# Moving a mixture-of-experts token gather and scatter from TensorE to indirect DMA through HBM

## The reference, cut to what matters

```python
def swiglu(h, wg, wu, wd):
    return (jax.nn.silu(h @ wg) * (h @ wu)) @ wd

def moe_swiglu(h, router, wg, wu, wd):          # h: (1, 256, 1024), wg, wu: (8, 1024, 3584), wd: (8, 3584, 1024)
    logits = (h @ router).astype(jnp.float32)
    top_val, top_idx = lax.top_k(logits, TOP_K)  # 2 of 8
    probs = jax.nn.softmax(top_val, axis=-1)
    combine = jnp.einsum('bske,bsk->bse', jax.nn.one_hot(top_idx, N_EXPERTS, dtype=jnp.float32), probs)
    out = jnp.zeros(h.shape, jnp.float32)
    for e in range(N_EXPERTS):
        out = out + combine[..., e:e + 1] * swiglu(h, wg[e], wu[e], wd[e]).astype(jnp.float32)
    return out.astype(h.dtype)
```

## Time and profile before

| | |
|---|---|
| median of 3 runs | 1943.22 us |
| profiled execution | 1944.21 us |
| its span | 1942.4 us |
| mean granted TensorE clock | 0.971 |
| PE, DVE, ACT busy over the span | 94%, 78%, 58% |
| HBM read, written | 483.31 MB, 1.05 MB |

### The profile page before, as it was taken

How to read it: one execution, slowest core, us unless ns; L and a number is a source line. 1 busy time by engine, 2 the same in 40 slices (tenths; PEclk the granted TensorE clock), 3 DMA queues, 4 the chain that set the end, 5 groups by cost and what they waited for, 6 DMA issues and landing times.

```text
span 1942.4 us, 27834 instructions
## 1 busy us (share of the span) xinstructions
PE 1817.0 (94%) x10592; PEld 1594.6 (82%) x10592; DVE 1521.2 (78%) x1487; ACT 1131.6 (58%) x923; POOL 5.1 (0%) x13
## 2 busy tenths in 40 slices
PE   6889899899988898897999999999999999999996
PEld 6888788799978897785788888888888888888885
DVE  3989967544548899576788989889898898988995
ACT  3345545444334355543576767777677776776774
POOL 0000000000000000000000000000000000000000
PEclk9999989999989999998899999999999999999998
DMA  6444333765334444335699999999999999999992
GB/s 235 137 146 153 130 98 129 249 195 186 117 122 143 136 141 148 109 131 184 215 381 338 359 359 364 363 340 357 363 362 353 348 360 377 344 355 347 369 367 90
DMA packets 234304, 485.51 MB, mean 250 GB/s; under 512 B 19040, under 2 KB 43616, under 8 KB 234096
## 3 DMA queue, kind: packets, MB, share of 16 engines
q1 hardware_dynamic: 233168, 479.65, 70.0%
q0 software_dynamic: 1056, 4.76, 0.6%
HBM read 483.31 MB, written 1.05 MB: 249 GB/s over the span
## 4 chain that ended last, share of the span: by engine, by line
PE 74%; DVE 19%; ACT 4%; DMA 2%; issue 1%; SPq 0%; DVEq 0%; ACTq 0%
PE pair L833 48%; PE aux L833 19%; DVE lo_ring L1315 6%; DVE arena L1378 5%; PE aux L1206 2%; ACT hi_ring L450 1%; PE pair L1228 1%; PE aux L1279 1%; DMA raw_ring<-in_w_in 1%; DVE arena L1547 1%; DVE arena L1496 1%; DVE arena L1482 1%; DVE small L1495 1%; DVE pair L1472 1%; DVE arena L1561 0%
## 5 line engine op out<-in xcount | busy, mean ns | idle before, releaser
L1315 DVE TENSOR_TENSOR lo_ring<-raw_ring,hi_ring 128x2048 fp32r<-128x2048 f32 (+2 forms) x278 | 623.3, 2246 | 139.0 <-ACT hi_ring L450 137.1
L450 ACT ACTIVATE hi_ring<-raw_ring 128x2048 fp32r<-128x2048 f32 (+2 forms) x278 | 522.5, 1881 | 298.5 <-PE pair L833 214.8
L1315 DVE TENSOR_TENSOR lo_ring<-arena,hi_ring 128x2048 fp32r<-128x2048 f32 x183 | 417.7, 2289 | 98.9 <-ACT hi_ring L450 97.4
L450 ACT ACTIVATE hi_ring<-arena 128x2048 fp32r<-128x2048 f32 x183 | 350.3, 1918 | 152.5 <-PE aux L833 81.4
L833 PE MATMUL pair<-hT_lo,hi_ring 128*128 128x256 f32 (+1 forms) x1360 | 396.5, 292 | 28.7 <-DVE lo_ring L1315 14.3
L833 PE MATMUL pair<-hT_hi,lo_ring 128*128 128x256 f32 (+1 forms) x1360 | 391.3, 288 | 0.0
L833 PE MATMUL pair<-hT_hi,hi_ring 128*128 128x256 f32 (+1 forms) x1360 | 391.1, 288 | 0.0
L833 PE MATMUL pair<-lo_ring,hT_hi 128*128 128x512 f32 x896 | 355.5, 397 | 3.9 <-DVE hT_lo L1820 2.4
L833 PE MATMUL pair<-hi_ring,hT_hi 128*128 128x512 f32 x896 | 350.1, 391 | 0.0
L833 PE MATMUL pair<-hi_ring,hT_lo 128*128 128x512 f32 x896 | 349.8, 390 | 0.0
L833 PEld LDWEIGHTS pair<-hT_lo,hi_ring 128*128 128x128 f32 (+1 forms) x1360 | 267.1, 196 | 36.4 <-issue 13.9
(11 more groups left out here) (285 smaller groups left out, 1895.8 us busy)
## 6 DMA issues: line engine op xcount, KB each, us to landing
raw_ring<-in_mu SPq DMA_DIRECT2D x222, 512.0 KB, 5.8
arena<-in_mg SPq DMA_DIRECT2D x220, 512.0 KB, 5.4
raw_ring<-in_w_in SPq DMA_DIRECT2D x120, 512.0 KB, 4.5
arena<-in_md SPq DMA_DIRECT2D x114, 512.0 KB, 5.5
raw_ring<-in_md SPq DMA_DIRECT2D x110, 512.0 KB, 5.5
raw_ring<-in_w_br SPq DMA_DIRECT2D x32, 512.0 KB, 4.5
raw_ring<-in_w_out SPq DMA_DIRECT2D x16, 512.0 KB, 4.2
raw_ring<-in_fg SPq DMA_DIRECT2D x12, 512.0 KB, 4.1
```

Of the source, the lines that this page charges most:

```text
L450: nc.scalar.activation(hi_ring[:, h, 0:cols], raw(slot)[:, 0:cols], ACT.Copy).then_inc(hi_ready, 1)
L1315: nc.vector.tensor_tensor(lo_ring[:, h, 0:cols], raw(slot)[:, 0:cols], hi_ring[:, h, 0:cols].bitcast(f32), ALU.subtract).then_inc(lo_ready, 1)
```

## The change

All rounds but the first now take their tokens out of HBM, and all but the last give their result to HBM. Two tensors of 384 rows x 1024 are added in HBM: `rows` (the 256 normed tokens and 128 spare rows) and `sums` (x, and 128 spare rows), filled from SBUF by four DMAs on the POOL queue after the last norm. `fetch(j)` on POOL is an indirect DMA that reads 128 rows of `rows` into `arena` (`A_ROWS`); `put(j)` is an indirect DMA that adds 128 rows of `arena` (`A_OUT`) into `sums`. The row numbers of each round are one column of `place`. A token position that no token fills points to a spare row. TensorE turns the fetched rows with 8 transposes (`turn_rows`) in step 5 instead of the gather, and DVE scales the round's result by its weights out of `aux` into `A_OUT` in step 1 (`output`), with no split, scatter or add. Before the last scatter, `sums` is read back into x.

The row numbers are found once: DVE makes the 0/1 matrices of all 12 slots (24 compares, L1877 of the changed kernel), TensorE multiplies them by a three-column table of token number, one and weight (`index_slots`, 24 matmuls in float32, after the first `exp_up`), and DVE turns the result into `place` and `wts` (`places`, four small operations). The last round keeps the old way out: `turn_pick`, `pickT_copy`, output split and scatter, now once, with the second token block's scatter going to `pair0` instead of waiting for `aux`.

The diff, cut to its core:

```diff
+A_ROWS, A_OUT = 7680, 8704
+A_PICKS = A_OUT
+ROWS = T + 128
...
+            pool.wait_ge(S["normed"], 8)
+            pool.dma_start(rows_d[0:T, :].rearrange("(b p) d -> p b d", p=128), hN).then_inc(rows_kept, 16)
+            pool.dma_start(sum_d[0:T, :].rearrange("(b p) d -> p b d", p=128), x[:, :, :]).then_inc(rows_kept, 16)
+            pool.dma_start(rows_d[T:ROWS, :], x[:, 0, :]).then_inc(rows_kept, 16)
+            pool.dma_start(sum_d[T:ROWS, :], x[:, 0, :]).then_inc(rows_kept, 16)
+
+            def fetch(j):
+
+                nc.gpsimd.tensor_copy(place_in[:, :], place[:, bass.ds(j, 1)]).then_inc(S["place_in_set"], 1)
+                pool.wait_ge(S["place_in_set"], j)
+                pool.sem_inc(pool_ready, 1)
+                pool.indirect_dma_start(ar(A_ROWS, D), None, rows_d, bass.IndirectOffsetOnAxis(ap=place_in[:, :], axis=0))\
+                    .then_inc(rows_in, 16)
+
+            def put(j):
+
+                nc.gpsimd.tensor_copy(place_out[:, :], place[:, bass.ds(j, 1)]).then_inc(S["place_out_set"], 1)
+                pool.wait_ge(S["place_out_set"], j + 1)
+                pool.wait_ge(S["out_scaled"], j + 1)
+                pool.sem_inc(pool_ready, 1)
+                pool.indirect_dma_start(sum_d, bass.IndirectOffsetOnAxis(ap=place_out[:, :], axis=0), ar(A_OUT, D), None,
+                                        compute_op=ALU.add).then_inc(sums_added, 16)
+
+            pool.wait_ge(rows_kept, 64)
+            pool.wait_ge(S["places_done"], 1)
+            fetch(1)
+
+            def slot(j):
+                pool.wait_ge(S["gathered"], j + 1)
+                fetch(j + 1)
+                if not (isinstance(j, int) and j == 1):
+                    pool.wait_ge(sums_added, 16 * j - 16)
+                put(j - 1)
+
+            slot(1)
+            with pool.Fori(2, NE) as j:
+                slot(j)
+            pool.wait_ge(S["meta_done"], 1)
+            m = pool.value_load(meta[0:1, 0:1], min_val=0, max_val=EXTRA)
+            with pool.If(m > 0):
+                with pool.Fori(NE, m + NE) as j:
+                    slot(j)
+            pool.wait_ge(sums_added, 16 * m + 16 * (NE - 1))
+            pool.sem_inc(pool_ready, 1)
+            pool.dma_start(x[:, :, :], sum_d[0:T, :].rearrange("(b p) d -> p b d", p=128)).then_inc(sums_in, 16)
...
-                    if s == 1 and not first:
-                        output_hi(j - 1, EXP_BASE + exp_at(j * EXP_STEPS, 5) + 1)
...
-                    if s == 3:
-                        pickT_copy(j)
...
+            pickT_copy()
+            output_hi(EXP_BASE + exp_at(exp_end, 1) + 1)
...
-            def gather(j):
-
-                pe.wait_ge(S["pick_done"], j + 1)
+            def gather_first():
+
+                pe.wait_ge(S["pick_done"], 1)
                 for k in range(KT):
                     for b in range(NB):
                         for n, src in enumerate((act_lo, act_hi)):
                             ins = pe.matmul(aux[:, 1024 + k * 128:1024 + (k + 1) * 128], src[:, b * D + k * 128:b * D + (k + 1) * 128],
                                             pick[:, b, :], start=(b == 0 and n == 0), stop=(b == 1 and n == 1))
+                ins.then_inc(S["gathered"], 1)
+
+            def index_slots():
+
+                pe.wait_ge(S["picks_done"], 1)
+                for c in range(SLOTS):
+                    for b in range(NB):
+                        ins = pe.matmul(aux[:, 1024 + 3 * c:1027 + 3 * c], ar(A_PICKS + (c * NB + b) * 128, 128),
+                                        ar(A_SCORE + 240 + (b * SLOTS + c) * 3, 3), start=(b == 0), stop=(b == 1))
+                ins.then_inc(S["indexed_slots"], 1)
+
+            def turn_rows(j):
+                pe.wait_ge(rows_in, 16 * j)
+                for k in range(KT):
+                    ins = pe.transpose(aux[:, 1024 + k * 128:1024 + (k + 1) * 128], ar(A_ROWS + k * 128, 128), C("ident"))
...
-            def turn_pick(j, first):
-                if not first:
-                    pe.wait_ge(S["x_added"], 2 * j)
+            def turn_pick():
+                pe.wait_ge(S["pick_done"], 2)
                 for b in range(NB):
-                    ins = pe.matmul(aux[:, 1024 + b * 128:1152 + b * 128], pick[:, b, :], ident_r[:, :], start=True, stop=True)
+                    ins = pe.matmul(pairs[0][:, b * 128:(b + 1) * 128], pick[:, b, :], ident_r[:, :], start=True, stop=True)
...
+                    if s == 0 and first:
+                        index_slots()
+                    if s == 5:
+                        turn_rows(j + 1)
                     if s == 1 and not first:
-                        scatter(j - 1, 0)
-                    if s == 3:
-                        turn_pick(j, first)
-                    if s == 5:
-                        pe.wait_ge(S["pickT_done"], j + 1)
-                        gather(j + 1)
+                        pe.wait_ge(S["out_scaled"], j)
                     if s:
                         exp_down(n, 4, s - 1)
                     elif not first:
                         exp_down(n, 4, EXP_STEPS - 1)
...
-                    if s == 1 and not first:
-                        scatter(j - 1, 1)
                     exp_turn(n)
 
-            def scatter(j, b):
-
-                if b == 0:
-                    pe.wait_ge(S["oe_lo_done"], j + 1)
-                else:
-                    pe.wait_ge(S["x_added"], 2 * j + 1)
-                for half in range(2):
-                    for n, src in enumerate((oel, oeh)):
-                        ins = pe.matmul(aux[:, 1024 + half * 512:1536 + half * 512], pickT[:, b, :],
-                                        src[:, half * 512:(half + 1) * 512], start=(n == 0), stop=(n == 1))
-                ins.then_inc(S["scattered"], 1)
+            def scatter():
+
+                pe.wait_ge(S["oe_lo_done"], 1)
+                pe.wait_ge(S["pickT_done"], 1)
+                for b in range(NB):
+                    for half in range(2):
+                        out = aux[:, 1024 + half * 512:1536 + half * 512] if b == 0 else pairs[0][:, half * 512:(half + 1) * 512]
+                        for n, src in enumerate((oel, oeh)):
+                            ins = pe.matmul(out, pickT[:, b, :], src[:, half * 512:(half + 1) * 512], start=(n == 0), stop=(n == 1))
+                    ins.then_inc(S["scattered"], 1)
...
+            turn_pick()
             exp_down((m + NE) * EXP_STEPS, 0, EXP_STEPS - 1)
-            scatter(m + (NE - 1), 0)
-            scatter(m + (NE - 1), 1)
+            scatter()
...
+            for c in range(SLOTS):
+                for b in range(NB):
+                    ins = nc.vector.tensor_scalar(ar(A_PICKS + (c * NB + b) * 128, 128), C("iota"), pos_t[:, b, c:c + 1], None,
+                                                  ALU.is_equal)
+            tok = ar(A_SCORE + 240, NB * SLOTS * 3).rearrange("p (b c k) -> p b c k", b=NB, k=3)
+            at = CONSTS["place"][0]
+            for b in range(NB):
+                nc.vector.tensor_copy(tok[:, b, :, 0:1], consts[:, at + b:at + b + 1].unsqueeze(1).broadcast_to([128, SLOTS, 1]))
+            nc.vector.memset(tok[:, :, :, 1:2], 1.0)
+            nc.vector.tensor_copy(tok[:, :, :, 2:3], comb_t[:, :, :].unsqueeze(3)).then_inc(S["picks_done"], 1)
...
-                        output_lo(j - 1)
-                    if s == 4:
-                        dve.wait_ge(S["pickT_done"], j + 1)
-                        make_pick(j + 1)
+                        output(j - 1, EXP_BASE + exp_at(n - 1, 5) + 1)
                     exp_lo(n, 3)
                     if not opening:
                         exp_lo(n, 4)
                         exp_lo(n, 5)
                     exp_hid(n)
-                    if s == 1 and not first:
-                        add(j - 1, 0)
-                    if s == 2 and not first:
-                        add(j - 1, 1)
+                    if s == 0 and first:
+                        places()
...
+            wts = ar(A_SCORE + 320, SLOTS)
+
+            def places():
+                dve.wait_ge(S["indexed_slots"], 1)
+                got = aux[:, 1024:1024 + 3 * SLOTS].rearrange("p (c k) -> p c k", k=3)
+                spot = ar(A_SCORE + 336, SLOTS).unsqueeze(2)
+                link(nc.vector.tensor_copy(spot, got[:, :, 0:1]))
+                link(nc.vector.scalar_tensor_tensor(spot, got[:, :, 1:2], consts[:, at + 2:at + 3],
+                                                    spot, ALU.mult, ALU.add))
+                link(nc.vector.tensor_scalar(place[:, :], ar(A_SCORE + 336, SLOTS), consts[:, at + 3:at + 4], None, ALU.add))
+                nc.vector.tensor_copy(wts.unsqueeze(2), got[:, :, 2:3]).then_inc(S["places_done"], 1)
+                dve.wait_ge(S["places_done"], 1)
+
+            def output(j, used):
+
+                dve.wait_ge(panel_used, used)
+                if not (isinstance(j, int) and j == 0):
+                    dve.wait_ge(sums_added, 16 * j)
```

(12 more changed lines are left out.)

32 lines of the change are left out of this document (19 added, 13 removed).

## The result

| | before | changed |
|---|---|---|
| time, median of 4 runs each on the same chip | 1945.2 us | 1916.41 us (1915.53 to 1918.58) |
| profiled execution, its span | 1944.21, 1942.4 us | 1916.89, 1914.4 us |
| HBM read, written | 483.31, 1.05 MB | 488.55, 7.86 MB |

The ratio is 0.9855, with a 95% interval of 0.9843 to 0.9867: 28.8 us faster by the medians, 27.3 by the profiled executions, 28.0 by their spans. Forecast were 28.0 and a time of 1915.

What follows compares the result with a forecast made beforehand. TensorE's own instruction list was taken to bound the rounds. From 1944.21 us, -38.1 + 5.0 + 5.5 + 1.5 - 1.9 gave 1916.2; with the median 1.0 below the profiled execution, 1915, range 1907 to 1935.

Steps and rivals of the forecast that it cites:

- (a): Opening: 24 compares and four small operations ahead of `hx_lo(0)` delay TensorE's first up product by 5.0 us (2.1 to 5.9).
- (b): Opening: `index_slots` after the first up product, 24 x 0.227 = 5.4 us, makes step 1 5.5 us later.
- (c): Opening: lower TensorE clock behind the grown gaps costs 1.5 us, taken between nothing and 2.9.
- the end: Last scatter: its second half follows the first directly in its own PSUM tile, matmuls 0.43 apart, 1.9 us less.
- What bounds a round: Rounds: TensorE's instruction list sets their length; net 4.99 us off rounds 1 to 7, 118.5 instead of 123.5.
- The transfers: Rounds: at 389 GB/s panels need 113.2 us; fetch 1.35 plus put 2.7 fit in the 5.3 left.
- B: Rival: transfers mildly bound the rounds, 118.5 to 121.35 us each; 1917 to 1935, typically 1926; chance 0.22.
- C: Rival: the adding put is dear; 8.0 us of all engines per put gives 1943, 10 us gives 1957; chance 0.09.
- D: Rival: the rounds' 357 GB/s is a ceiling, so a round takes 126.3 us, total 1971; chance 0.05.
- rival E: Rounds: DVE is held while POOL builds indirect transfers; 5 us per indirect DMA gives 1947, 3 us 1919; chance 0.04.

## Why the prediction was right, step by step

The spans differ by 28.0 us. Cut at events that both traces have:

| stretch | forecast | measured |
|---|---|---|
| up to the pick's compare (920.29, now 921.36) | 0 | +1.1 |
| (a) to the first up matmul (930.35, now 935.87) | +5.0 | +4.5 |
| (b), (c) to the gather or `turn_rows` of round 0 (1025.95, now 1038.02), less `turn_pick` | +6.5 | +6.6 |
| to the last `exp_down`'s last matmul (1923.85, now 1899.08) | -37.6 | -36.8 |
| the end | -1.9 | -3.2 |
| sum | -28.0 | -28.0 |

That the sums agree to the tenth is luck: the lines miss by 1.1, 0.5, 0.1, 0.8 and 1.3, and the misses cancel.

**What bounds a round.** Right, and this step carried the time. A round is TensorE's list: 118.59 measured against 118.5, 4.87 less against 4.99, and the 0.12 seven times is the 0.8 of the table. The experiments with one half of the change gave 120.84 and 121.36. That scatter and gather came off in full was shown; that nothing took their place was shown by leaving the transfers out (118.59 again).

**(a) The compares.** 0.200 us each (4.79 / 24), as taken. The four small operations overlapped more than priced, and 0.5 was over.

**(b) and (c).** Together 7.05 (the 6.55 and the 0.50 of `turn_pick`) against 7.0. Up to the first matmul of step 1 (947.39, now 958.01) it is 5.1 beyond (a), against the 5.5 of (b), and behind that matmul 1.95, against the 1.5 of (c). The product took 5.28 from its start to the transposes behind it (5.4 forecast). I had guessed half of a loss of 2.9 to the clock. It was at half twice, and only the second spell is new, since the first also ends at 936.4 before and moved with (a):

```profile
920.50:940.90 20.40, 12.09 (x44) 10.92 (x45) 15.93 (x77) 2.82 (x2) 0.00 (x0) 0.50 0.09 28
940.90:954.60 13.70, 13.70 (x87) 12.21 (x86) 2.98 (x2) 9.31 (x6) 0.00 (x0) 1.00 0.31 113
954.60:961.40 6.80, 4.39 (x13) 3.31 (x13) 6.54 (x7) 0.60 (x1) 4.40 (x2) 0.50 0.34 100
```

3.4 us of the second spell lie in step 1's up product (958.01 to 961.40), worth 1.7, near the 1.5. I had blamed the gap before step 1 for it. The version with `index_slots` one step later, where no gap is left, still fell to half for 3.4 us behind the product. So the reason given for (c) was wrong and its size near: what precedes the fall is the row of 48 narrow passes. In the changed kernel too the clock falls at 954.6, as the product ends and before the gap.

**The end.** Mis-sized: 3.2 instead of 1.9. The step kept the pace of before, matmuls 0.43 apart. That was half clock, from 1926.2 on, as this stretch of the kernel before shows; in the changed kernel the same stretch, from 1895.00 to 1906.50, has 1.00.

```profile
1926.20:1930.00 3.80, 2.08 (x4) 1.16 (x4) 1.52 (x2) 0.60 (x2) 0.00 (x0) 0.51 0.00 0
```

Nor does the new end bring the full clock with it. The kernel with the put alone has the same end and half clock in it (2.07 us for the first four scatter matmuls, 1.59 for the other four), and the kernel with the fetch alone has the old end and full clock for the first four (1.21). So the 1.3 us beyond the forecast are chance as far as these traces show; why the clock falls when it does was not tried.

**The first 1.1 us** come before any added instruction, and the four filling DMAs are not their cause. POOL issues these from 906.35 on (the rate from 904 to 914 is 405 GB/s), but ACT's first instruction of the last norm already starts at 900.19 where it was 899.03. In other kernels with the same filling DMAs the pick's compare starts between 918.99 (compares moved) and 921.92 (`places` later as well), so this is the scatter of the unchanged part from run to run.

**The transfers** (rivals B, C and D). The put's 2.7 us was the guess, and 2.7 to 2.8 the measurement. The room was larger than thought: some 394 GB/s instead of 389, so 1.3 us more in a round. D fell by the rate of whole rounds, 381 GB/s. The Trainium skill ("DMA: Bandwidth & Descriptors", Specifications) gives a limit of about 358 GB/s per core, worked out as half of what two cores share. Here one core runs, and it moved 381 over 118.6 us, so the figure is no ceiling for it. C was a true mechanism with a false price: with four adding stores a round the kernel is slower than before (1952.53).

**DVE held by POOL** (rival E). While POOL issues its indirect DMAs the low parts on DVE keep their 2.28 to 2.29 us, and with four stores in a row, 13.0 us of POOL in 120, the waits begin with DMA. The contention of which the Trainium skill speaks ("SBUF — State Buffer", Who interferes with whom) seems to be there, but it is POOL that waits. Each of POOL's small copies from `place` to `place_in` starts inside a low part of DVE, which has two SBUF inputs, and ends within 0.1 us of that low part's end:

```profile
955.78 2.22 POOL L451 COPY place_in<-place 128x1 uint32<-128x1 uint32 x1 [46.93 <-DVE arena L1943]
...
1274.44 2.29 DVE L1376 TENSOR_TENSOR lo_ring<-arena,hi_ring 128x2048 fp32r<-128x2048 f32 x1 [0.43 <-ACT hi_ring L504]
```

The first took 2.22 us beside the low part that starts at 955.66, the one at 1276.22 took 0.56 and ended at 1276.78, where this low part ended at 1276.73; the same copy into `place_out`, at 1280.41 with no low part under way, took 0.20. It costs nothing, since POOL has a round's time.

## What to carry to other kernels

Where one engine is busy all the time and the others wait for it, price its own list from the chain view and believe the sum, but bring moved work into a place where the other engines are ahead: the same row numbers cost 11 us where each engine waited for the other and 7 one or two steps later. Count a store that adds as two plain stores of the same bytes, and compare all engine time of a round with the round, not the landing time of one transfer. A DMA share near 1 is not a ceiling: it read 0.99 at 359 GB/s and 1.02 at 381; ask for the fastest stretch in the trace, and take that as a lower bound too.
